# Seven-product steps for six more column pairs, and the gates kept on chip, in a hybrid decoder block

## The chip, the cores and the metric

The kernel runs on one core of one Trainium2 chip. The metric is the device time of one execution in microseconds (us); the core has a matrix engine (TensorE, PE in the rows, PEld for its weight loads), VectorE (DVE), ScalarE (ACT), GpSimd (POOL) and SyncE (SP), whose queue issues nearly all weight transfers.

## The reference, cut to what matters

The block takes `x` of 256 rows by 2048 columns, all in float32.

```python
h = rmsnorm(x, norm_mix)
q, k, v, o_pre, i_pre, f_pre, cb, cc, cx, ga, gb = split_columns(h @ w_in)
hm = mlstm_chunkwise(q, k, v, i_pre + b_igate, f_pre + b_fgate)      # 8 heads of 256 columns
hm = hm * rsqrt(mean(hm * hm, per head) + EPS) * mh_norm
hm = sigmoid(o_pre) * hm
y_a = hm @ w_branch_a
y_b = (cb * causal_depthwise_conv(cc * cx, conv_w)) @ w_branch_b
merged = sigmoid(ga) * y_a + sigmoid(gb) * y_b
x = x + merged @ w_out
hf = rmsnorm(x, norm_ffn)
x = x + (silu(hf @ w_gate) * (hf @ w_up)) @ w_down
return rmsnorm(x, norm_final)
```

`o_pre`, `ga` and `gb` are 2048 columns wide each, and so are the weights of both branches and of the output projection, with 2048 rows each.

## The kernel before, in words

**Chunks.** All weights pass through one ring in chunks of 1 MB, 128 partitions of 2048 values. SP loads chunk after chunk into four slots of `w_raw`; a load waits until VectorE has split the chunk four places earlier (`lo_split`). ScalarE copies a chunk to `w_hi` in the type fp32r (`split`, the copy at L580), VectorE subtracts it from the raw values to get `w_lo` (`split`, L1029). Both have two slots: ScalarE may write a slot when TensorE has finished the first part of its work on the chunk two places earlier (`hi_used`), VectorE when TensorE has finished all of it (`lo_used`).

**Plain chunks.** A float32 product is made of three: `x_hi w_hi`, `x_lo w_hi`, `x_hi w_lo`. A chunk holds either four row blocks of 128 by 512 columns (`project`, L1666, L1667, L1675) or two row blocks by 1024 columns. With 256 rows of x, either is 8 block products of 128 x 128 by 512 columns, so 24 matmuls: 16 with `w_hi`, then 8 with `w_lo`.

**Seven-product steps.** `front_step` (L1759, L1760, L1766) works on pairs of 512-column blocks, a pair having 8 steps. In the steps named in `FRONT_S` it makes the 8 block products out of 7 (a Strassen-like scheme), so 21 matmuls. That needs sums of the tiles of x (`x_form_hi`, `x_form_lo`, made once by `x_forms` on VectorE) and sums of the weight blocks of that chunk: VectorE's `sums_of` (L1130, L1133, L1135), then ScalarE's copy to `t_hi_x`, then VectorE's `t_lo_x` (L1155). The products land in eight PSUM banks (`FRONT_BANKS`). `front_extra` (L1180 to L1185) takes four of them in step 7, once ScalarE has copied the bank P1; `front_main` (L1192) takes the other four after the pair, and ScalarE's `front_out` scales the four results with the rows' factor into `qk` or `vx`. Steps are called by pair and number below: (1, 2) is step 2 of pair 1.

**Order before.** Chunks follow this order: two plain blocks of q and k; three pairs (`FRONT` = 3: the rest of q and k, then v) with 2, 3 and 3 seven-product steps; four turns `conv_turn` of 12 plain chunks, one for each 512-column block of cb, cc, cx, with the recurrence of two heads woven in; four plain blocks of `o_pre`, 4 chunks each; four turns `merge_turn` of 16 plain chunks (ga, branch a, gb, branch b); four blocks of the output projection; then the FFN and the down projection, which use seven-product steps too. The last transposes and taps of the convolution (`turn_p`, `p_taken`, `conv_0`, `conv_1`, `cu_high`, `conv_low`) run during the first block of `o_pre`. There the Sigmoid of each block goes to `nat`, VectorE forms the gated heads `hm` (L1354), TensorE turns them (`turn_block`, L1684) and `group_hi` and `group_lo` store `hmT_hi`, `hmT_lo`. The order of each engine's work is written out by hand; a wait blocks everything behind it on its engine.

In the pairs ScalarE's loop has this body, which the change touches:

```python
if j < 2 * BC - 1:
    front_split(p, j + 1)
...
if p > 0 and j == 0:
    front_out(p - 1)
```

`front_out(p - 1)` waits for `front_main(p - 1)` of VectorE.

Of the kernel before, what the change touches and what calls it, by code (L numbers as in the profile page):

```python
# [29 lines left out]
ALU = mybir.AluOpType  # L30
# [20 lines left out]
FRONT_S = ((4, 6), (2, 4, 6), (2, 4, 6))  # L51
# [50 lines left out]
def hybrid_block(nc, x, norm_mix, w_in, b_igate, b_fgate, conv_w, mh_norm, w_branch_a, w_branch_b,  # L102
# [29 lines left out]
    G_MERGE = G_O + NB * BC  # L132
    G_OUT = G_MERGE + 4 * NB * BC
# [20 lines left out]
    with ExitStack() as ctx:  # L154
# [20 lines left out]
        hmT_hi, hmT_lo = at("hmT_hi", [P, KC, SEQ], F32R, R3), at("hmT_lo", [P, KC, SEQ], F32R, R3 + AT)  # L175
# [14 lines left out]
        actT = at("actT", [P, FC, SEQ], F32, Z)  # L190
# [14 lines left out]
        fT_hi, fT_lo = at("fT_hi", [P, KC, SEQ], F32R, R3), at("fT_lo", [P, KC, SEQ], F32R, R3 + AT)  # L205
# [18 lines left out]
        hm = at("hm", [P, RT, COLS], F32, s + 4096)  # L224
# [65 lines left out]
        def sem(name):  # L290
# [44 lines left out]
                                                                 sem("x_form_hi_done"), sem("x_form_lo_done"))  # L335
        xp1_out, x_extra, x_main = sem("xp1_out"), sem("x_extra"), sem("x_main")
# [17 lines left out]
        FRONT_AT = (G_QK + 2 * BC, G_V, G_V + 2 * BC)  # L354
        FRONT = len(FRONT_AT)
# [36 lines left out]
        def _(sp):  # L392
# [39 lines left out]
            for p, c in enumerate((C_QK + 2 * COLS, C_V, C_V + 2 * COLS)):  # L432
                for j in range(2 * BC):
                    chunk = Chunk(FRONT_AT[p] + j)
                    sp.wait_ge(lo_split, chunk.count(1 - RAW_SLOTS))
                    sp.dma_start(w_raw[:, chunk.raw, :].rearrange("p (k n) -> p k n", k=2),
                                 w_in_k[:, 2 * j:2 * j + 2, c:c + 2 * COLS]).then_inc(raw_landed[chunk.raw], 16)
            with sp.Fori(0, NB) as i:
# [60 lines left out]
        def _(pool):  # L499
# [50 lines left out]
            rstd_of(h_mean, ss[:], ss[:], rstd[:], 1, DV, h_rstd)  # L550
            pool.wait_ge(x1_summed, 1)
# [27 lines left out]
        def _(act):  # L579
# [22 lines left out]
            def group_hi(n, dst, k0, step, scale_at=None):  # L602

                act.wait_ge(grp_turned, n)
                src = bank_kt(4)
# [77 lines left out]
            def front_split(p, j):  # L683

                if j in FRONT_S[p]:
# [4 lines left out]
                    copy(t_hi_x[:], t_raw_x[:].rearrange("p u n -> p (u n)")).then_inc(t_hi_done, 1)  # L690
                split(Chunk(FRONT_AT[p] + j))

            def front_out(p):

                act.wait_ge(x_main, (p + 1) * X_MAIN)
                for b in range(2):
                    for r in range(RT):
                        if p == 0:
# [1463 lines left out]
```

## Time and profile before

| | |
|---|---|
| median of 3 runs | 1724.8 us (1724.71 to 1725.06) |
| the profiled execution's own time | 1725.06 us |
| its span, first to last instruction | 1723.2 us |
| TensorE busy | 1711.2 us, 99% of the span, 7724 matmuls |
| VectorE busy | 1181.7 us, 69% |
| ScalarE busy | 858.8 us, 50% |
| GpSimd busy | 61.7 us, 4% |
| mean granted TensorE clock | 0.998 |

The profile was taken in one execution; 1.9 us of its own time lie outside the span. Busy shares are averages over stages with different limits. TensorE's matmuls are pipelined: one is recorded as 0.39 us long while the next starts 0.23 us after it, so its rate is read from the distance between starts.

### The profile page before, as it was taken

The page shows a single profiled execution, that of the slowest core. Times are in us where ns is not written, and L with a number is a line of the kernel's source. Part 1 is how long each engine was busy: PE and PEld are TensorE (multiplying, and loading weights), DVE is VectorE, ACT ScalarE, POOL GpSimd, SP SyncE. Part 2 cuts the span into 40 slices and gives each one's busy share as a digit, 9 for nine tenths or more (in the row PEclk, how much of TensorE's full clock was granted, in tenths as well). Part 3 has the DMA queues.
Part 4 walks back from the last instruction along what each step waited for, and adds up shares of the span by engine and source line. Part 5 has one row for each costly group of instructions (what it writes and reads, how often), then busy time and mean ns, then how long its engine had stood idle before and what let it go on. Part 6 is the DMA issues. An engine that isn't in the chain of part 4 may idle for free.

```text
span 1723.2 us, 20654 instructions
## 1 busy us (share of the span) xinstructions
PE 1711.2 (99%) x7724; PEld 1418.9 (82%) x7724; DVE 1181.7 (69%) x991; ACT 858.8 (50%) x756; POOL 61.7 (4%) x60
## 2 busy tenths in 40 slices
PE   9999999999999999999999999999999999999998
PEld 8888888888888888888888888888888888888886
DVE  5888555566565544444445579888888888898887
ACT  6555544454444434333333556555555555555564
POOL 1000010101000000000000000000000000230000
PEclk9999999999999999999999999999999999999999
DMA  8555545554555555555556556655556565556653
GB/s 281 188 190 200 190 160 188 171 167 161 181 180 186 177 194 193 195 195 195 195 195 233 182 171 197 199 201 200 201 196 196 197 199 201 184 195 222 221 195 118
DMA packets 151465, 331.29 MB, mean 192 GB/s; under 512 B 8720, under 2 KB 8816, under 8 KB 151024
## 3 DMA queue, kind: packets, MB, share of 16 engines
q1 hardware_dynamic: 151264, 329.98, 56.6%
q8 instruction: 38, 0.62, 0.1%
q10 hardware_dynamic: 144, 0.52, 0.1%
q14 instruction: 19, 0.16, 0.0%
HBM read 328.38 MB, written 2.10 MB: 192 GB/s over the span
## 4 chain that ended last, share of the span: by engine, by line
PE 98%; issue 0%; DVE 0%; ACT 0%; DMA 0%; SPq 0%; POOLq 0%; DVEq 0%; POOL 0%; ACTq 0%
PE ps L1666 16%; PE ps L1667 16%; PE ps L1675 16%; PE ps L1989 9%; PE ps L1991 9%; PE ps L1995 9%; PE ps L2070 4%; PE ps L2071 4%; PE ps L2075 4%; PE ps L1759 2%; PE ps L1760 2%; PE ps L1766 2%; PE ps L1684 1%; PE ps L1945 1%; PE ps L1796 0%
## 5 line engine op out<-in xcount | busy, mean ns | idle before, releaser
L1029 DVE TENSOR_TENSOR w_lo<-w_raw,w_hi 128x2048 fp32r<-128x2048 f32 x308 | 709.7, 2307 | 239.8 <-ACT w_hi L580 237.1
L580 ACT ACTIVATE w_hi<-w_raw 128x2048 fp32r<-128x2048 f32 (+1 forms) x309 | 588.8, 1910 | 311.3 <-PE ps L1667 171.8
L1666 PE MATMUL ps<-w_hi,xT_hi 128*128 128x512 f32 x832 | 329.7, 396 | 0.0
L1667 PE MATMUL ps<-w_hi,xT_lo 128*128 128x512 f32 x832 | 324.0, 389 | 0.0
L1675 PE MATMUL ps<-w_lo,xT_hi 128*128 128x512 f32 x832 | 205.6, 389 | 0.0
L1675 PEld LDWEIGHTS ps<-w_lo,xT_hi 128*128 128x128 f32 x832 | 156.2, 188 | 32.4
L1666 PEld LDWEIGHTS ps<-w_hi,xT_hi 128*128 128x128 f32 x832 | 156.3, 188 | 32.2
L1667 PEld LDWEIGHTS ps<-w_hi,xT_lo 128*128 128x128 f32 x832 | 156.3, 188 | 31.5
L1989 PE MATMUL ps<-w_hi,fT_hi 128*128 128x512 f32 x396 | 156.3, 395 | 0.0
L1991 PE MATMUL ps<-w_hi,fT_lo 128*128 128x512 f32 x396 | 154.3, 390 | 0.0
L580 ACT ACTIVATE t_hi<-t_raw 128x1536 fp32r<-128x1536 f32 x45 | 66.9, 1486 | 110.4 <-PE ps L1995 87.8
L1995 PE MATMUL ps<-w_lo,fT_hi 128*128 128x512 f32 x396 | 120.1, 389 | 0.0
L2070 PE MATMUL ps<-w_hi,a_hi 128*128 128x512 f32 x280 | 109.0, 389 | 0.0
L2071 PE MATMUL ps<-w_hi,a_lo 128*128 128x512 f32 x280 | 108.9, 389 | 0.0
L1995 PEld LDWEIGHTS ps<-w_lo,fT_hi 128*128 128x128 f32 x396 | 74.3, 188 | 15.4
L1989 PEld LDWEIGHTS ps<-w_hi,fT_hi 128*128 128x128 f32 x396 | 74.4, 188 | 15.0 <-issue 0.3
L1991 PEld LDWEIGHTS ps<-w_hi,fT_lo 128*128 128x128 f32 x396 | 74.4, 188 | 14.8
L1397 DVE TENSOR_TENSOR t_lo<-t_raw,t_hi 128x1536 fp32r<-128x1536 f32 x33 | 57.9, 1756 | 23.0 <-ACT t_hi L580 22.9
L2075 PE MATMUL ps<-w_lo,a_hi 128*128 128x512 f32 x280 | 73.3, 389 | 0.1
L1989 PE MATMUL ps<-w_hi,form_hi 128*128 128x512 f32 x176 | 68.6, 390 | 0.0
L1991 PE MATMUL ps<-w_hi,form_lo 128*128 128x512 f32 x176 | 68.5, 389 | 0.0
L2075 PEld LDWEIGHTS ps<-w_lo,a_hi 128*128 128x128 f32 x280 | 52.5, 188 | 11.4 <-DVE w_lo L1029 0.5
(295 smaller groups left out, 2345.8 us busy)
## 6 DMA issues: line engine op xcount, KB each, us to landing
w_raw<-in_w_in SPq DMA_DIRECT2D x127, 1024.0 KB, 5.1
w_raw<-in_w_gate SPq DMA_DIRECT2D x88, 512.0 KB, 3.8
w_raw<-in_w_up SPq DMA_DIRECT2D x88, 512.0 KB, 4.6
w_raw<-in_w_down SPq DMA_DIRECT2D x44, 1024.0 KB, 5.3
w_raw<-in_w_branch_a SPq DMA_DIRECT2D x16, 1024.0 KB, 5.0
w_raw<-in_w_branch_b SPq DMA_DIRECT2D x16, 1024.0 KB, 5.0
w_raw<-in_w_out SPq DMA_DIRECT2D x16, 1024.0 KB, 5.1
xn<-in_x SPq DMA_DIRECT2D x4, 512.0 KB, 8.4
```

The source lines that it names most:

```text
L580: copy = lambda o, i, **kw: nc.scalar.activation(o, i, ACT.Copy, **kw)
L1029: V.tensor_tensor(w_lo[:, chunk.split, :], w_raw[:, chunk.raw, :], w_hi[:, chunk.split, :].bitcast(F32), ALU.subtract).then_inc(lo_split, 1)
L1397: V.tensor_tensor(t_lo[:], t_raw[:].rearrange("p u n -> p (u n)"), t_hi[:].bitcast(F32), ALU.subtract).then_inc(t_lo_done, 1)
L1666: T.matmul(ps[:, banks + r, :], rows(hi, k, r), w, start=(q == 0 and k == 0), stop=False)
L1667: last = T.matmul(ps[:, banks + r, :], rows(lo, k, r), w, start=False, stop=False)
L1675: last = T.matmul(ps[:, banks + r, :], rows(hi, k, r), w, start=False, stop=(q == BC - 1 and k == KB - 1))
L1989: T.matmul(ps[:, banks[name], :], tile_of(0, k, tile), moving(0, u), start=begins(name) and part is own(name)[0], stop=False)
L1991: return T.matmul(ps[:, banks[name], :], tile_of(1, k, tile), moving(0, u), start=False, stop=False)
L1995: return T.matmul(ps[:, banks[name], :], tile_of(0, k, tile), moving(1, u), start=False, stop=final(name) and part is own(name)[-1])
L2070: T.matmul(ps[:, banks[name], :], tile(0, t), moving(0, u), start=start, stop=False)
L2071: return T.matmul(ps[:, banks[name], :], tile(1, t), moving(0, u), start=False, stop=False)
L2075: return T.matmul(ps[:, banks[name], :], tile(0, t), moving(1, u), start=False, stop=stop)
```

## The change: what it does

The four blocks of `o_pre`, `ga` and `gb` become six pairs (numbers 3 to 8) that run through `front_step`, two for each. Pair 3 has seven-product steps 4 and 6; pairs 4 to 8 have steps 2, 4 and 6. The 16 + 64 chunks of the old blocks become 48 chunks in pairs and 32 plain ones of the branches, now without loops in the program. The sums of x for the later pairs are made again by GpSimd (`late_x_forms`), split by ScalarE in pair 3 at j = 2 and by VectorE at j = 3. ScalarE applies the Sigmoid in `front_out`; the eight gate blocks of ga and gb stay in SBUF. VectorE gates the heads in place in `vx` during pairs 4 and 5 (`gate_heads`), and TensorE turns them (`turn_heads`) in the first four plain chunks, which are of branch b. `front_out` is cut in two halves, issued at j = 1 and 2 of the next pair, for the three old pairs as well (after the third: at j = 0 and 1 of the convolution). Several tensors get other places in SBUF.

```diff
-FRONT_S = ((4, 6), (2, 4, 6), (2, 4, 6))
+FRONT_S = ((4, 6), (2, 4, 6), (2, 4, 6), (4, 6)) + ((2, 4, 6),) * 5
+FRONT = 3
...
@@ SyncE
-            with sp.Fori(0, NB) as i:
-                load_block(G_O, i, BC, w_in_k, C_O + i * COLS)
-            with sp.Fori(1, NB + 1) as i:
-                for n, (w, c) in enumerate(((w_in_k, C_GA), (w_a_k, 0), (w_in_k, C_GB), (w_b_k, 0))):
-                    load_block(G_MERGE + (n - 4) * BC, i, 4 * BC, w, i * COLS + (c - COLS))
+            for n, c in enumerate((C_O, C_O + 2 * COLS, C_GA, C_GA + 2 * COLS, C_GB, C_GB + 2 * COLS)):
+                load_x_pair(FRONT + n, c)
+            for i in range(NB):
+                for n, w in enumerate((w_b_k, w_a_k)):
+                    load_block(G_Y + (2 * i + n) * BC, 0, 0, w, i * COLS)
@@ GpSimd, after rstd_of(h_mean, ...)
+            def late_x_forms():
+                nc.gpsimd.tensor_tensor(out=late_pick[:], in0=steps(xT_hi), in1=steps(xT_lo),
+                                        op=ALU.add).then_inc(late_form_step, 1)
+                pool.wait_ge(late_form_step, 1)
+                for n in range(2):
+                    nc.gpsimd.tensor_tensor(out=late_form_raw[:, :, n, :], in0=late_pick[:, :, 0, n * P:(n + 1) * P],
+                                            in1=late_pick[:, :, n, P:2 * P] if n else late_pick[:, :, 0, P:2 * P],
+                                            op=ALU.subtract).then_inc(late_form_step, 1)
+                ... (two more of the same size)
@@ ScalarE
-            def front_out(p):
+            def front_out(p, b):
                 act.wait_ge(x_main, (p + 1) * X_MAIN)
...
+                    last = nc.scalar.activation(dst, src, ACT.Copy if p < FRONT else ACT.Sigmoid,
+                                                scale=r_x[:, 0, r:r + 1])
...
-                    if p > 0 and j == 0:
-                        front_out(p - 1)
+                    if p > 0 and j in (1, 2):
+                        front_out(p - 1, j - 1)
...
+            for p in range(FRONT, PAIRS):
+                for j in range(2 * BC):
+                    if j < 2 * BC - 1:
+                        front_split(p, j + 1)
...
+                    if p == FRONT and j == 0:
+                        p_taken(NB - 1)
+                    if p == FRONT and j == 2:
+                        cu_high(NB - 1)
+                        act.wait_ge(late_form_step, 5)
+                        copy(late_forms[0][:], late_form_raw[:]).then_inc(x_form_hi_done, 1)
+                    if p > FRONT and j in (1, 2):
+                        front_out(p - 1, j - 1)
@@ VectorE
+            def gate_heads(n, b, r):
+                dve.wait_ge(act_out, A_O + 2 * n + b + 1)
...
+                for k in range(2):
+                    h = 4 * n + 2 * b + k
+                    part = vx[:, r, h, 0:DV]
+                    last = V.scalar_tensor_tensor(out=part, in0=part, scalar=rstd[:, r * H + h:r * H + h + 1],
+                                                  in1=c_o[b][:, r, k * DV:(k + 1) * DV], op0=ALU.mult, op1=ALU.mult)
...
+            for p in range(FRONT, PAIRS):
+                for j in range(2 * BC):
+                    if j == FRONT_S[p][-1] + 1:
+                        front_extra(p)
+                    if j > 0 and j + 2 in FRONT_S[p]:
+                        front_sums(p, j + 2)
+                    if p == FRONT and j == 3:
+                        dve.wait_ge(x_form_hi_done, 2)
+                        V.tensor_tensor(late_forms[1][:], late_form_raw[:], late_forms[0][:].bitcast(F32),
+                                        ALU.subtract).then_inc(x_form_lo_done, 1)
+                    if j < 2 * BC - 1:
+                        front_split(p, j + 1)
...
+                    if p in (FRONT + 1, FRONT + 2) and 3 <= j < 7:
+                        gate_heads(p - FRONT - 1, (j - 3) // 2, (j - 3) % 2)
+                    if p == FRONT and j < 3:
+                        (conv_0, conv_1, conv_low)[j](NB - 1)
+                front_main(p)
@@ TensorE
+            for p in range(FRONT, PAIRS):
+                for j in range(2 * BC):
...
+                    if p > FRONT and j == 0:
+                        pe.wait_ge(x_extra, p * X_EXTRA)
+                    if p > FRONT and j == FRONT_S[p][0]:
+                        pe.wait_ge(x_main, p * X_MAIN)
+                    front_step(p, j)
+                    if p == FRONT and j == 0:
+                        turn_p(NB - 1)
+            for i in range(NB):
+                for j in range(2 * BC):
+                    n, q = j // BC, j % BC
...
+                    project(Chunk(G_Y + i * 2 * BC + j), 2 * n, *((cuT_hi, cuT_lo), (hmT_hi, hmT_lo))[n], q)
...
+                        turn_heads(q, 4 + q % 2 * 2)
+                    if i > 0 and j == 1:
...
+                        turn_block(gate_a[i - 1], 4, grp_turned)
```

## Rows read from the trace of the kernel before

**Rows 1.** The page: busy time of each engine; the group of ScalarE's chunk copies.

```profile
PE 1711.2 (99%) x7724; PEld 1418.9 (82%) x7724; DVE 1181.7 (69%) x991; ACT 858.8 (50%) x756; POOL 61.7 (4%) x60
...
L580 ACT ACTIVATE w_hi<-w_raw 128x2048 fp32r<-128x2048 f32 (+1 forms) x309 | 588.8, 1910 | 311.3 <-PE ps L1667 171.8
```

**Rows 2.** Waits of TensorE: us in total, times, longest.

```profile
PE ps L1759 <- issue: 0.8, 2, 0.4
```

**Rows 3.** Windows: us; busy of PE, PEld, DVE, ACT, POOL; clock; DMA; GB/s.

```profile
482.10:926.50 444.40, 444.40 (x1994) 368.61 (x1993) 220.14 (x139) 180.44 (x131) 0.00 (x0) 1.00 0.55 191
134.80:176.80 42.00, 41.58 (x184) 34.15 (x183) 35.48 (x29) 22.16 (x17) 0.00 (x0) 1.00 0.57 197
1037.00:1079.40 42.40, 42.40 (x190) 34.90 (x189) 39.39 (x32) 25.96 (x18) 0.00 (x0) 1.00 0.65 217
```

**Rows 4.** Timeline of TensorE, first matmuls of steps (0, 4), (0, 5), (0, 6).

```profile
82.74 0.39 PE L1759 MATMUL ps<-w_hi,xT_hi 128*128 128x512 f32 x1
...
87.50 0.39 PE L1759 MATMUL ps<-w_hi,xT_hi 128*128 128x512 f32 x1
...
92.94 0.39 PE L1759 MATMUL ps<-w_hi,xT_hi 128*128 128x512 f32 x1
```

**Rows 5.** Timeline of TensorE, end of step (1, 1), start of (1, 2).

```profile
112.21 1.97 PE L1766 MATMUL ps<-w_lo,xT_hi 128*128 128x512 f32 x8
114.60 0.47 PE L1759 MATMUL ps<-w_hi,xT_hi 128*128 128x512 f32 x1 [0.42 <-issue]
114.91 0.40 PE L1760 MATMUL ps<-w_hi,xT_lo 128*128 128x512 f32 x1
```

**Rows 6.** Timeline of ScalarE in steps (1, 1) and (1, 2).

```profile
108.75 2.56 ACT L580 ACTIVATE qk<-c_x,r_x 128x512 f32<-128x512 f32 x4 [5.25 <-DVE c_x L1192]
111.22 1.47 ACT L580 ACTIVATE t_hi_x<-t_raw_x 128x1536 fp32r<-128x1536 f32 x1
```

**Rows 7.** Timeline of VectorE from step (0, 7) to (1, 2).

```profile
98.79 0.69 DVE L1180 TENSOR_TENSOR c_x<-ps,c_x 128x512 f32<-128x512 f32 x1 [3.17 <-ACT c_x L580]
...
101.45 2.28 DVE L1029 TENSOR_TENSOR w_lo<-w_raw,w_hi 128x2048 fp32r<-128x2048 f32 x1
103.65 1.22 DVE L1130 TENSOR_TENSOR t_raw_x<-w_raw 128x1024 f32<-128x1024 f32 x1
...
106.24 2.48 DVE L1192 TENSOR_TENSOR c_x<-ps,c_x 128x512 f32<-128x512 f32 x4
108.63 2.28 DVE L1029 TENSOR_TENSOR w_lo<-w_raw,w_hi 128x2048 fp32r<-128x2048 f32 x1
112.72 1.76 DVE L1155 TENSOR_TENSOR t_lo_x<-t_raw_x,t_hi_x 128x1536 fp32r<-128x1536 f32 x1 [1.81 <-ACT t_hi_x L580]
```

**Rows 8.** Timeline of TensorE, `w_lo` part of the third chunk of `o_pre`.

```profile
497.39 1.98 PE L1675 MATMUL ps<-w_lo,xT_hi 128*128 128x512 f32 x8
```

**Rows 9.** Timeline of VectorE in the first blocks of `o_pre`.

```profile
496.72 1.23 DVE L1246 TENSOR_TENSOR uT<-uT,cbT 128x1024 f32<-128x1024 f32 x1
497.86 2.28 DVE L1029 TENSOR_TENSOR w_lo<-w_raw,w_hi 128x2048 fp32r<-128x2048 f32 x1
...
507.49 1.68 DVE L1354 SCALAR_TENSOR_TENSOR hm<-vx,rstd,nat 128x256 f32<-128x256 f32 x4 [4.00 <-ACT nat L597]
```

**Rows 10.** Timeline of ScalarE in the same place.

```profile
497.98 1.07 ACT L580 ACTIVATE cuT_hi<-uT 128x1024 fp32r<-128x1024 f32 x1 [3.40 <-DVE uT L1246]
```

**Rows 11.** Timeline of GpSimd, before `o_pre` and in the down projection.

```profile
476.05 2.92 POOL L520 TENSOR_TENSOR rstd<-ss,half 128x16 f32<-128x16 f32 x1
...
1484.46 0.74 POOL L562 TENSOR_TENSOR down_form_raw<-actT 128x256 f32<-128x256 f32 x1
1485.28 0.46 POOL L565 TENSOR_TENSOR down_form_raw<-down_form_raw,actT 128x128 f32<-128x128 f32 x1
...
1498.03 2.19 POOL L562 TENSOR_TENSOR down_form_raw<-actT 128x256 f32<-128x256 f32 x1 [11.31 <-DVE down_form_lo L1553]
1500.30 2.39 POOL L565 TENSOR_TENSOR down_form_raw<-down_form_raw,actT 128x128 f32<-128x128 f32 x1
```

More of the change, by code:

```diff
@@ L760, in conv_turn @@
                     split(c.next())
-                    if j == 0 and first:
-                        front_out(FRONT - 1)
+                    if j in (0, 1) and first:
+                        front_out(FRONT - 1, j)
                     if j == 0 and not first:
@@ L807, in _ @@
                 conv_turn(i)
-            for n in range(NB):
-                for q in range(BC):
-                    c = Chunk(G_O + n * BC + q)
-                    split(c.next())
-                    if n == 0:
-                        if q == 0:
-                            p_taken(NB - 1)
-                        if q == 2:
-                            cu_high(NB - 1)
-                    if n > 0 and q == 1:
-                        group_hi(GRP_HM + n, hmT_hi, (n - 1) * KB, 0, V_MH)
-                if n > 0:
-                    act.wait_ge(hm_done, n)
-                else:
-                    act.wait_ge(p_turned, NB)
-                take(c, n % 2, nat[:], ACT.Sigmoid)
@@ L828, in merge_turn @@
-            def merge_turn(i):
-                first = starts(i)
-                for j in range(4 * BC):
-                    c = Chunk(G_MERGE + j, i, 4 * BC)
-                    split(c.next())
-                    if j == 1:
-                        if first:
-                            group_hi(GRP_M, hmT_hi, (NB - 1) * KB, 0, V_MH)
-                        else:
-                            group_hi(i + GRP_M, mT_hi, (i - 1) * KB, 0)
-                    if j == 3:
-                        if not first:
-                            act.wait_ge(dve_out, V_MERGE + i * 2)
-                        take(c, 0, gate[:], ACT.Sigmoid)
-                    if j == 3 + 2 * BC:
-                        act.wait_ge(dve_out, V_MERGE + 1 + i * 2)
-                        take(c, 0, gate[:], ACT.Sigmoid)
@@ L851, in pair_split @@
+            for i in range(NB):
+                for j in range(2 * BC):
+                    split(Chunk(G_Y + i * 2 * BC + j).next())
+                    if i == 0 and j in (1, 2):
+                        front_out(PAIRS - 1, j - 1)
+                    if i == 0 and j < BC:
+                        group_hi(GRP_HM + j + 1, hmT_hi, j * KB, V_MH, 4 + j % 2 * 2)
+                    if i > 0 and j == 1:
+                        group_hi(GRP_M + i, mT_hi, (i - 1) * KB)
             def pair_split(j, i):
@@ L891, in _ @@
                     if n == 0 and q == 1:
[L892 removed]
+                        group_hi(GRP_F, mT_hi, (NB - 1) * KB)
                     if n > 0 and q == 0:
@@ L1379, in merge_turn @@
                 dve.wait_ge(dve_out, V_MERGE + 2 + i * 2)
-                V.tensor_tensor(merged[:], merged[:], prod[:], ALU.add).then_inc(m_done, 1)
-            merge_turn(0)
-            with dve.Fori(1, NB) as i:
-                merge_turn(i)
+                V.tensor_tensor(gate_a[i][:], gate_a[i][:], gate_b[i][:], ALU.add).then_inc(m_done, 1)
             def pair_split(j, i):
```

290 lines of the change are left out of this document (147 added, 143 removed).

## The prediction, on record before the changed kernel ran

> **What bounds the kernel now.** The page comes first: TensorE is busy for 1711.2 of 1723.2 us, in 7724 matmuls, and no other engine for more than 69% [rows 1]. The waits of TensorE come next, since a busy engine may still be slowed by others: what bears on this change is one entry, two waits that start at L1759, so in the pairs [rows 2]. The windows say whether the region to be changed is different: from 482.1 to 926.5 us, where `o_pre` and the branches are computed, TensorE is busy all the time at granted clock 1.00 (the higher of its two levels, 2.4 GHz), and VectorE for 220 of 444 us [rows 3]. So the time goes by the number of matmuls, and work added on VectorE is free until it makes TensorE wait. For the price of a matmul I take starts, not durations: the seven-product step (0, 4) runs from 82.74 to 87.50, 4.76 us for 21 matmuls, and the plain step (0, 5) to 92.94, 5.44 us for 24 [rows 4]. Both are 0.2267 us for one matmul, whichever tiles it reads.
>
> **Matmuls removed.** 80 chunks stay 80 chunks, and 17 of them lose 3 matmuls each: 51 x 0.2267 = 11.56 us, all on the path. Transposes stay as many: 8 for `turn_p`, 32 for the heads, 32 for `merged`. That sum is the firm part.
>
> **The two waits in the old pairs.** In step (1, 1) the last eight matmuls start at 112.21 and every 0.2267 us after it, so that step (1, 2) could start at 114.02. It starts at 114.60, and its second matmul comes 0.31 instead of 0.23 us later: 0.66 us lost [rows 5]. ScalarE shows why: it waited 5.25 us for VectorE's last results of pair 0, copied them for 2.56 us in `front_out`, and only then made the `t_hi` of step (1, 2), at 111.22, and behind it the chunk's `w_hi` [rows 6]. The changed order puts `t_hi` and `w_hi` of step 2 ahead of `front_out`. The sums of the weights are done at 106.24 [rows 7], so `t_hi` ends at 107.7 and, with 1.91 us for a chunk [rows 1], `w_hi` at 109.6, long before 114.02. VectorE then goes on at 110.9 instead of idling 1.81 us [rows 7]. The wait is there twice [rows 2]; both go: 1.32 us. Bounds: 0, if VectorE and not the order were to blame, and 1.32.
>
> **VectorE in the new pairs.** A whole old pair costs it 35.48 us [rows 3]. The gated heads add 8 operations to pairs 4 and 5; four of them took 1.68 us [rows 9], so 3.4 us, together 38.8 us. A pair with three seven-product steps has 183 matmuls, 41.5 us. That is a load of 94%; a turn of the FFN runs at 39.39 of 42.4 us, 93%, without holding TensorE up [rows 2, 3]. The order inside a pair matters more than the sum. From the old pair: `front_extra` can start 0.9 us after TensorE is done with step 6 (98.79) and ends at 101.45; then come a split, the sums (103.65 to 106.24), `front_main` (2.48 us) and the split of step 1, which ends at 110.9 [rows 7]. TensorE starts (1, 1) at 108.58 (one plain step before 114.02) and wants `w_lo` 16 matmuls later, at 112.2: 1.3 us to spare. In the steps after it each split is ready with more than that. The gating comes when VectorE idled in the old pair (1.81 us at once at 112.72, 3.17 us before 98.79). I take 0 for pairs 4 to 8; the upper bound is 0.66 us for each, the wait of rows 5.
>
> **Where pair 3 begins.** Here three things meet on VectorE: the last taps of the convolution, the sums for step (3, 4), and the `lo` part of the new forms. The chunks keep their places up to there. The third chunk's `w_lo` part starts at 497.39 [rows 8], so (3, 3) runs from 499.20 to 504.64 and wants `w_lo` at 502.83. VectorE ends the last convolution product so that its next operation starts at 497.86 [rows 9]. Before, this was the split of (3, 3); now the sums are first, 2.59 us (103.65 to 106.24), to 500.45, and the split ends at 502.73 [rows 7], 0.1 us before it is wanted. Then `conv_low`, of the size of the product at 496.72, with 1.14 us from start to start [rows 9], to 503.8; the forms' `lo`, as large as `t_lo` and so 1.76 us [rows 7], to 505.55. ScalarE is earlier: `cu_high` ends at 499.05 [rows 10], the forms' copy and `t_hi` take 1.47 each [rows 6] and `w_hi` 1.91 [rows 1], to 503.9. So (3, 4) starts 0.91 us late, plus 0.08 us for the start as in rows 5: first wait, 1.0 us. Its `w_hi` part is 14 matmuls, 3.17 us, so `w_lo` and `t_lo` are wanted at 508.8. VectorE ends `t_lo` at about 507.2 and the split at 509.4: second wait, 0.7 us. What is late next: the sums of step (3, 6) end at 512.0 and the split of (3, 5) at 514.2; TensorE, at (3, 5) from about 511.1, wants it at 514.7. From there VectorE is in front again. Together 1.7 us. Bounds: 0, if each overlaps a little better, and 6.1 us, if none of the added work ahead of that split (2.59 + 1.76 + 1.76) is hidden.
>
> **GpSimd's new forms.** One operation over 1536 columns and four over 384, after `rstd`, which ends at 478.97 [rows 11]. ScalarE asks for them at 499.05. Cheap, with VectorE out of the way, 256 columns took 0.74 and 128 took 0.46 us [rows 11], so 2.2 ns for a column and 0.18 us for an operation: 7.7 us, done at 487. If each also waits for one split of VectorE, 5 x 2.28 more, they end at 498. I take 0. Rows 11 show the dear end too: the 128 columns take 2.39 us while VectorE is at its SBUF operations. The Trainium skill, SBUF — State Buffer, Who interferes with whom, has the rule that speaks against moving such work: a VectorE instruction with two SBUF inputs and a GpSimd instruction that reads SBUF exclude each other for the whole instruction. By that the trace agrees (2.39 against 0.46 us), and five such waits give the 498 above, so the sum would stay.
>
> **The rest, at nothing.** The Sigmoids are as many as before, 24, and ScalarE has half of each window free [rows 3]. The weights of a pair are 8.4 MB in 41.5 us, 202 GB/s, where the FFN's window moved 217 with TensorE busy throughout [rows 3]. In the first plain chunks ScalarE has 1.91 us of copy in each 5.44 us [rows 1, 4], and beside it the two halves of `front_out` (2.56 us together [rows 6]) and the four groups of `group_hi`; a group stored late holds TensorE only from the fifth chunk on, where branch a begins to read the turned heads.
>
> **Sum.** 1725.06 (the profiled execution) - 11.56 - 1.32 + 1.7 = 1713.9 us. The median of the runs is 0.26 us below that execution, so **1713.6 us**.
>
> **Rivals.** *The start of pair 3 is covered.* VectorE's margin there is tenths; if the forms' `lo` comes in time, 1725.06 - 12.88 = 1712.2, median 1711.9 us. Against it: the operations are in series and none can be left out. 15%. *The feeders are late in every pair.* If VectorE, at 94%, and not `front_out`'s place causes the waits of rows 5, the old two stay and the five later pairs have one each: -11.56 + 1.7 + 5 x 0.66 = -6.6, 1718.2 us. For it: the margin of 1.3 us in step 1. Against it: ScalarE's 5.25 us of idling ahead of `front_out` [rows 6]. 15%. *GpSimd is late, and the kernel slower.* At the dearest row, 2.39 us for 128 columns, the 3072 columns of the forms take 57.4 us and end at 536.3. ScalarE, held in pair 3 at j = 2 with the copies of (3, 4) behind it, needs 4.85 us more, so TensorE starts at 541.2 instead of 504.6: 36.5 us lost, 1725.06 - 12.88 + 36.5 = 1748.7, median 1748.4 us. It decides from forms that end at 512.7 (no gain left) and is a measurable loss from 516.1. Against it: VectorE is busy half of that stretch [rows 3], and the cheap rows are a fifth of the dear one. 3%. The forecast as worked out has 57%; 10% lies between it and the second rival, with a longer wait at pair 3.
>
> **How the numbers follow.** Likeliest: 1713.6. Range: the first rival with half a microsecond below, 1711.2, up to 1717.5, which takes in most of the 6.1 us bound at pair 3 and leaves out the two rivals above it, 18%. Within 0.2% (3.4 us), about what a measurement of this kernel can tell from no change, lies only GpSimd's lateness in part: faster 95%, same 2%, slower 3%.
>
> **What would show it.** Right: 7673 matmuls; no wait of TensorE at steps (1, 2) and (2, 2); one of about 1.0 and one of about 0.7 us at (3, 4), put down to VectorE's forms and splits; starts 0.2267 us apart and clock 1.00 throughout the pairs; GpSimd's forms done before 499. Wrong: waits at step 1 or 2 of pairs 4 to 8, starts further apart in steps that read `late_form_hi`, transposes of the heads that wait for `hm_done`, or group stores in the branch chunks that hold TensorE.

## The result, and the profile after

| | before | changed |
|---|---|---|
| median | 1724.76 us (1724.56 to 1725.06, 4 runs) | 1713.72 us (1713.38 to 1714.92, 4 runs) |
| the profiled execution's own time | 1725.06 us | 1713.56 us |
| its span | 1723.2 us | 1711.7 us |
| matmuls | 7724 | 7673 |

The changed kernel takes 0.9937 of the time before (95% interval 0.992 to 0.9954), so it is 11.0 us faster. The forecast was 1713.6 us, and it rested on a sum of three terms. A sum can come out right with wrong terms, so the two traces are compared stage by stage.

The page of the changed kernel, its line of busy times; [rows 1] has the one of before:

```profile
PE 1698.0 (99%) x7673; PEld 1407.2 (82%) x7673; DVE 1281.9 (75%) x1108; ACT 888.0 (52%) x780; POOL 71.3 (4%) x65
```

TensorE has 51 matmuls fewer. VectorE has 100 us more work and ScalarE 29 us more, and neither has become the bound: the page says so, but only a stage's waits prove it. The waits of TensorE in the changed kernel (line waited at, whom for, us in total, times, longest):

```profile
PE ps L1754 <- POOL half L523: 1.7, 1, 1.7
PE ps L1713 <- ACT w_hi L616: 1.7, 1, 1.7
PE ps L1814 <- ACT w_hi L616: 0.9, 1, 0.9
PE ps L1759 <- DMA vec_rows<-in_conv_w: 0.7, 1, 0.7
PE ps L1821 <- DVE w_lo L1064: 0.4, 1, 0.4
```

The first, second and fourth lie in the first 30 us, in code that is as before, and vary from run to run by half a microsecond and more. L1814 and L1821 are `front_step` after the change. The two waits of [rows 2] are gone, and in their place stand one of 0.9 and one of 0.4 us. The view of TensorE over time says where (start, duration, operation, what ended the idle time):

```profile
191.14 0.61 PE L1886 MATMUL ps<-ident,r_a 8*128 8x8 f32 x4
...
500.99 2.08 PE L1821 MATMUL ps<-w_lo,xT_hi 128*128 128x512 f32 x8
503.96 0.47 PE L1814 MATMUL ps<-w_hi,xT_hi 128*128 128x512 f32 x1 [0.90 <-ACT w_hi L616]
504.27 0.40 PE L1815 MATMUL ps<-w_hi,xT_lo 128*128 128x512 f32 x1
...
507.01 0.39 PE L1815 MATMUL ps<-late_t_hi,xT_lo 128*128 128x512 f32 x1
507.75 0.50 PE L1821 MATMUL ps<-w_lo,xT_hi 128*128 128x512 f32 x1 [0.35 <-DVE w_lo L1064]
...
912.95 0.39 PE L1713 MATMUL ps<-w_hi,mT_hi 128*128 128x512 f32 x1
```

Both waits are at step (3, 4). Idle times in such rows are short by the modelled ends of the matmuls, so starts are compared: 507.01 to 507.75 is 0.74 us where 0.227 is the rule, and the start after it (508.09) comes 0.34 us later where 0.227 is the rule, so the wait cost 0.51 + 0.11 = 0.62 us. The first one, counted in the same way from the last matmul of the eight, which starts at 502.68, cost 1.06 + 0.08 = 1.14 us. Another 0.08 us is lost at the `w_lo` part at 500.99, whose second matmul comes 0.31 us after the first. Together 1.84 us.

With the first and last row of this fence (the first transposes of the head columns, where the convolution begins, and the first matmul of the output projection) and with the first matmul of `o_pre` the kernel falls into stages. The same landmarks are at 193.01, 481.98 and 924.46 us before, and at 191.14, 480.14 and 912.95 us after:

| stage, us | before | after | difference |
|---|---|---|---|
| first weight matmul (10.29, 9.79) | | | -0.50 |
| to the convolution: plain blocks, pairs 0 to 2 | 182.72 | 181.35 | -1.37 |
| convolution | 288.97 | 289.00 | +0.03 |
| `o_pre`, branches, gates | 442.48 | 432.81 | -9.67 |
| from the output projection to the last matmul | 789.96 | 790.03 | +0.07 |

The third difference is -51 x 0.2267 + 1.84 = -9.72, and 0.05 from many small steps. Of the -1.37, the two waits of [rows 5] are 1.32. The 0.50 us at the top is no part of the change: in the executions of this document the first weight matmul starts anywhere from 9.14 to 10.29 us. Without it the stages add up to -10.94 us, beside -11.04 for the medians.

### The profile page after: what moved, and what is told of

It reads as the page before. It is cut to its first block, busy times and chain, and to the rows that moved or that the text cites. A ratio compares the mean times of both kernels' runs of the same rounds, so it can differ in the third digit from the quotient of the medians.

```text
span 1711.7 us, 20301 instructions
## 1 busy us (share of the span) xinstructions
PE 1698.0 (99%) x7673; PEld 1407.2 (82%) x7673; DVE 1281.9 (75%) x1108; ACT 888.0 (52%) x780; POOL 71.3 (4%) x65
## 4 chain that ended last, share of the span: by engine, by line
PE 97%; DVE 1%; issue 1%; ACT 0%; DMA 0%; SPq 0%; POOLq 0%; DVEq 0%; POOL 0%; ACTq 0%
PE ps L1713 11%; PE ps L1714 11%; PE ps L1722 11%; PE ps L2032 9%; PE ps L2034 9%; PE ps L2038 9%; PE ps L1821 7%; PE ps L1814 7%; PE ps L1815 7%; PE ps L2113 4%; PE ps L2114 4%; PE ps L2118 4%; PE ps L1739 1%; PE ps L1988 1%; DVE w_lo L1064 0%
## 5 line engine op out<-in xcount | busy, mean ns | idle before, releaser
L1713 PE MATMUL ps<-w_hi,xT_hi 128*128 128x512 f32 x448 | 179.6, 401 | 1.7 <-ACT w_hi L616 1.7
L1714 PE MATMUL ps<-w_hi,xT_lo 128*128 128x512 f32 x448 | 174.6, 390 | 0.0
L1814 PE MATMUL ps<-w_hi,xT_hi 128*128 128x512 f32 x426 | 165.9, 389 | 0.9 <-ACT w_hi L616 0.9
L1815 PE MATMUL ps<-w_hi,xT_lo 128*128 128x512 f32 x426 | 165.7, 389 | 0.0
L1821 PE MATMUL ps<-w_lo,xT_hi 128*128 128x512 f32 x426 | 112.5, 390 | 0.4 <-DVE w_lo L1064 0.4
L1722 PE MATMUL ps<-w_lo,xT_hi 128*128 128x512 f32 x448 | 110.7, 389 | 0.0
L1713 PEld LDWEIGHTS ps<-w_hi,xT_hi 128*128 128x128 f32 x448 | 84.2, 188 | 19.3 <-ACT w_hi L616 1.9
L1722 PEld LDWEIGHTS ps<-w_lo,xT_hi 128*128 128x128 f32 x448 | 84.1, 188 | 17.5
L1714 PEld LDWEIGHTS ps<-w_hi,xT_lo 128*128 128x128 f32 x448 | 84.2, 188 | 16.8
L1814 PEld LDWEIGHTS ps<-w_hi,xT_hi 128*128 128x128 f32 x426 | 80.0, 188 | 17.8 <-issue 1.3
L1821 PEld LDWEIGHTS ps<-w_lo,xT_hi 128*128 128x128 f32 x426 | 79.9, 188 | 17.5 <-DVE w_lo L1064 1.0
L1815 PEld LDWEIGHTS ps<-w_hi,xT_lo 128*128 128x128 f32 x426 | 80.0, 188 | 16.5
```

What stands on the lines that cost most here:

```text
L1713: T.matmul(ps[:, banks + r, :], rows(hi, k, r), w, start=(q == 0 and k == 0), stop=False)
L1714: last = T.matmul(ps[:, banks + r, :], rows(lo, k, r), w, start=False, stop=False)
L1722: last = T.matmul(ps[:, banks + r, :], rows(hi, k, r), w, start=False, stop=(q == BC - 1 and k == KB - 1))
L1814: T.matmul(ps[:, banks[name], :], tile(0, t), moving(0, u), start=begins, stop=False)
L1815: last = T.matmul(ps[:, banks[name], :], tile(1, t), moving(0, u), start=False, stop=False)
L1821: last = T.matmul(ps[:, banks[name], :], tile(0, t), moving(1, u), start=False, stop=ends)
```

## The experiments

Each table or sentence gives the median of the kernel's own runs beside the ratio to the kernel before on the same chip. "C to D" is the stage from the first matmul of `o_pre` to the first of the output projection, 432.81 us in the changed kernel and 442.48 before; "A to B" is that from the first weight matmul to the convolution. A to B also holds the last of the first loads, which cost TensorE up to 1.2 us more in some executions (1.11 us at 15.39 in that with `front_out` whole and first), so it is compared only where they did not.

### The changed kernel again

> The changed kernel itself, on the chip of the runs sent with it: 1713.7 us, with the two waits at (3, 4) that together cost 1.8 us.

1713.98 us (1713.17 to 1714.17, 5 runs), ratio 0.9936 (0.9923 to 0.995). The waits at (3, 4) cost 1.14 and 0.62 us and A to B is 181.34 us, so both are properties of the order of work and not of one execution.

### Only the place and halves of front_out, in the kernel before

```diff
-def front_out(p):
+def front_out(p, b):
...
-    if p > 0 and j == 0:
-        front_out(p - 1)
+    if p > 0 and j in (1, 2):
+        front_out(p - 1, j - 1)
...
-    if j == 0 and first:
-        front_out(FRONT - 1)
+    if j in (0, 1) and first:
+        front_out(FRONT - 1, j)
```

> The kernel before with one part of the change alone: front_out in two halves, at j = 1 and 2 of the next pair (j = 0 and 1 of the convolution). If front_out's place caused the waits at steps (1, 2) and (2, 2), both go and the time falls by 1.3 to 1.4 us, to 1723.4, with t_hi of step (1, 2) ending about 5 us earlier. If VectorE's load caused them, they stay and the time stays at 1724.8.

1723.35 us (1722.62 to 1724.01, 11 runs), ratio 0.9994 (0.9985 to 1.0003). Over whole runs the effect is no larger than the uncertainty. The stage shows it: A to B falls from 182.72 to 181.33 us, by 1.39, and C to D stays at 442.48. ScalarE and TensorE of this kernel, in pair 1:

```profile
105.44 1.49 ACT L580 ACTIVATE t_hi_x<-t_raw_x 128x1536 fp32r<-128x1536 f32 x1 [2.85 <-DVE t_raw_x L1134]
```

```profile
111.30 1.98 PE L1765 MATMUL ps<-w_lo,xT_hi 128*128 128x512 f32 x8
113.11 0.39 PE L1758 MATMUL ps<-w_hi,xT_hi 128*128 128x512 f32 x1
```

`t_hi_x` no longer stands behind 2.56 us of `front_out`; it starts as soon as the sums are there, 4.9 us earlier than in [rows 6] when both are counted from the first weight matmul (9.39 and 10.29), and step (1, 2) starts 1.81 us = 8 x 0.2267 after the eight matmuls of [rows 5] began: no wait.

### The changed kernel with front_out whole and first again

```diff
-if p > 0 and j in (1, 2):
-    front_out(p - 1, j - 1)
+if p > 0 and j == 0:
+    front_out(p - 1, 0)
+    front_out(p - 1, 1)
```

(and the same for `p > FRONT` in the loop of the new pairs).

> The changed kernel with front_out whole at j = 0 again in all pairs. If its place is the cause, TensorE waits 0.66 us at step 2 of pairs 1, 2 and 4 to 8, seven times, and the time is 4.6 us above the changed kernel's 1713.7, at 1718.3. If VectorE's load were the cause in the old kernel, the place would change nothing: 1713.7.

1718.33 us (1718.04 to 1719.04, 5 runs), ratio 0.9964 (0.995 to 0.9977). C to D grows by 3.43 us, 0.69 for each of pairs 4 to 8, and the profile counts seven waits at the start of step 2. The waits of TensorE, and its rows at (4, 2):

```profile
PE ps L1816 <- issue: 2.9, 7, 0.4
```

```profile
536.13 1.97 PE L1823 MATMUL ps<-w_lo,xT_hi 128*128 128x512 f32 x8
538.52 0.47 PE L1816 MATMUL ps<-w_hi,xT_hi 128*128 128x512 f32 x1 [0.41 <-issue]
```

ScalarE in the same stretch:

```profile
532.67 2.57 ACT L741 ACTIVATE c_o<-c_o,r_x 128x512 f32<-128x512 f32 x4 [3.95 <-DVE c_o L1232]
```

536.13 to 538.52 is 2.39 us where 1.81 is the rule. It is the picture of [rows 5, 6] in every pair. So this small edit of the diff carries 0.65 to 0.69 us for each of seven pairs, 1 and 2 among them; without it the new pairs would have given back a third of their gain (3.43 of 9.67 us). The entry names "issue", which is what a wait looks like when the profile finds no event for it; ScalarE's row beside it names the cause.

### Pairs 4 to 8 with two seven-product steps

```diff
-FRONT_S = ((4, 6), (2, 4, 6), (2, 4, 6), (4, 6)) + ((2, 4, 6),) * 5
+FRONT_S = ((4, 6), (2, 4, 6), (2, 4, 6), (4, 6)) + ((4, 6),) * 5
```

> The changed kernel with steps 4 and 6 alone in pairs 4 to 8: 12 seven-product steps instead of 17. If a step is worth exactly its 3 matmuls and nothing is given back, the time rises by 5 x 0.68 = 3.4 us to 1717.1, with the same two waits at (3, 4). If VectorE held the pairs up, fewer steps would give part of it back and the rise would be under 2.5 us.

1717.37 us (1716.31 to 1718.35, 5 runs), ratio 0.9958 (0.9944 to 0.9972), 7688 matmuls. C to D grows by 3.41 us; 15 matmuls of 0.2267 us are 3.40. So the third step of these pairs gives its whole price back even in pairs 4 and 5, where VectorE has most to do. If VectorE had been costing TensorE something there, taking 5 sums and splits away would have saved some of it.

### The new sums of x made and split earlier

GpSimd makes the forms during the convolution; ScalarE copies them and VectorE splits them at the top of pair 3.

```diff
-            pool.wait_ge(h_squared, RT * H)
-            rstd_of(h_mean, ss[:], ss[:], rstd[:], 1, DV, h_rstd)
...
+            pool.wait_ge(staged, 2 * NB)
             late_x_forms()
+            pool.wait_ge(h_squared, RT * H)
+            rstd_of(h_mean, ss[:], ss[:], rstd[:], 1, DV, h_rstd)
...
                     if p == FRONT and j == 0:
+                        act.wait_ge(late_form_step, 5)
+                        copy(late_forms[0][:], late_form_raw[:]).then_inc(x_form_hi_done, 1)
                         p_taken(NB - 1)
...
+                    if p == FRONT and j == 0:
+                        dve.wait_ge(x_form_hi_done, 2)
...
+                        V.tensor_tensor(late_forms[1][:], late_form_raw[:], ...)
```

(and both are taken out of their old places, j = 2 and j = 3).

> The changed kernel with GpSimd's forms made right after the last staging of q and k (about 70 us earlier), ScalarE's copy of them ahead of p_taken and VectorE's lo part ahead of conv_0, where both engines were idle. If the waits at (3, 4) come from VectorE's chain of operations in series, taking 1.7 us out of it removes the first wait and all but about 0.1 us of the second: 1.7 us less than the changed kernel, 1712.0. If they come from something else (the landing of the chunk, ScalarE, PSUM banks), the time stays at 1713.7.

1712.22 us (1711.81 to 1713.49, 5 runs), ratio 0.993 (0.9916 to 0.9943). C to D falls by 1.77 us to 431.04. VectorE of this kernel:

```profile
484.01 1.75 DVE L1410 TENSOR_TENSOR late_form_lo<-late_form_raw,late_form_hi 128x1536 fp32r<-128x1536 f32 x1
```

The 1.75 us now lie in the time in which VectorE waits for ScalarE anyway (3.45 us of that wait are left, up to 489.21), and at 501.98, where the changed kernel has them, comes `late_t_lo`. TensorE starts step (3, 4) 1.91 us after the `w_lo` part of (3, 3) and waits no more. The edit moves three things at once (GpSimd's forms, ScalarE's copy, VectorE's subtraction); that the two waits of 1.76 us together hang on VectorE's operation of 1.75 us is read from the order in which TensorE's waits ended, told in the part on the prediction.

### As that, with the sums for step (3, 4) first as well

```diff
-if j > 0 and j + 2 in FRONT_S[p]:
+if j > 0 and j + 2 in FRONT_S[p] and not (p == FRONT and j + 2 == FRONT_S[p][0]):
     front_sums(p, j + 2)
...
+                        front_sums(p, FRONT_S[p][0])      # pair 3, j == 0, behind the split of the forms
```

> The kernel with early forms (e4), and VectorE's weight sums of step (3, 4) ahead of conv_0 too, in the place where it still idles for 3.45 us. They take 2.6 us out of the chain ahead of step (3, 4). If early forms left nothing but hundredths there (0.08 us at the w_lo part of (3, 3)), the time from the first matmul of pair 3 to the first of the output projection falls from 431.04 us by 0.1 us, and the median does not move beyond its noise: 1712.1.

**1711.83 us** (1711.78 to 1712.43, 5 runs), ratio 0.9927 (0.9914 to 0.9941). C to D is 430.91 us, which is 442.48 - 51 x 0.2267 = 430.92: nothing of the 51 matmuls is lost. It is the fastest version of all that ran, though against the one before it only the stage tells (0.13 us), not the runs.

### An 18th seven-product step, (3, 2)

The same early forms; the sums for step 2 at j = 0, and `conv_1`, `conv_low` and `cu_high` moved to j = 3, 5 and 4.

```diff
-FRONT_S = ((4, 6), (2, 4, 6), (2, 4, 6), (4, 6)) + ((2, 4, 6),) * 5
+FRONT_S = ((4, 6), (2, 4, 6), (2, 4, 6)) + ((2, 4, 6),) * 6
```

> The kernel with early forms, and step (3, 2) a seven-product step too, its sums ahead of conv_0; conv_1 and conv_low go to j = 3 and 5, cu_high to j = 4. Three matmuls fewer, 0.68 us; against it t_hi of (3, 2) is made behind p_taken, so w_hi of that step ends about 0.5 us after TensorE wants it, and VectorE's split of (3, 5) about 0.2 us. So about even with the 1712.2 of early forms: 1712.0 to 1712.4. If neither wait appears, 1711.5.

1712.57 us (1711.98 to 1712.71, 5 runs), ratio 0.9928 (0.9915 to 0.9942), 7670 matmuls. C to D is 430.93 us, 0.11 less than with 17 steps and the forms early. TensorE at (3, 2):

```profile
490.80 1.98 PE L1824 MATMUL ps<-w_lo,xT_hi 128*128 128x512 f32 x8
493.22 0.47 PE L1817 MATMUL ps<-w_hi,xT_hi 128*128 128x512 f32 x1 [0.44 <-issue]
```

Three matmuls saved are 0.68 us; the step starts 2.42 us after the `w_lo` part before it instead of 1.81, and its second matmul 0.08 us late: 0.69 us. ScalarE has `p_taken` (`pT` and `uT`, from 487.34 to 489.69) ahead of this step's `late_t_hi`, as it had `front_out` in [rows 6], and its `w_hi` behind that; another order was not tried. The step pays nothing as long as the wait is there.

### More load on VectorE in pairs 4 to 8

The added operation, of 128 x 768, computes nothing that is used. By the windows the three take 2.2 to 2.4 us of a pair: 11.05 us over the five, and 38.05 - 35.66 = 2.39 in pair 7, where TensorE never waits.

```diff
+                    if p > FRONT and j in (3, 4, 5):
+                        dve.wait_ge(pad_step, 3 * (p - FRONT - 1) + j - 3)
+                        V.tensor_tensor(pad[:].rearrange("p (k t) -> p k t", k=3), xT_lo[:, 0:3, :].bitcast(F32),
+                                        xT_lo[:, 3:6, :].bitcast(F32), ALU.add).then_inc(pad_step, 1)
```

> The changed kernel with three more VectorE additions of 128x768 (about 0.9 us each, into an unused place) in each of pairs 4 to 8, at j = 3, 4 and 5. VectorE's sum in pairs 4 and 5 becomes 41.7 us of a pair's 41.5, in pairs 6 to 8 38.3 us. If only the sum counts, TensorE waits under 1 us in all: 1713.7 to 1714.7. If the order inside a pair counts (rival: VectorE late at 92% already), each of the five pairs has waits and the time is 1717 or more.

1715.18 us (1715.03 to 1715.48, 4 runs), ratio 0.9945 (0.9929 to 0.996). C to D grows by 1.19 us: a little more than the 1 us at most that was expected if only the sum counted, and far less than the 3.3 us of waits in every pair. Busy time in windows of one pair, first of the changed kernel (TensorE, its weight loads, VectorE, ScalarE, GpSimd, granted clock, DMA share, GB/s), then of this kernel for VectorE alone:

```profile
525.80:567.30 41.50, 41.50 (x185) 34.38 (x184) 38.60 (x37) 23.82 (x17) 0.00 (x0) 1.00 0.58 203
...
608.80:650.30 41.50, 41.50 (x185) 34.38 (x184) 35.66 (x29) 22.42 (x16) 0.00 (x0) 1.00 0.57 203
```

```profile
526.80:568.30 41.50, 39.52 (x39) 1.00 0.59 203
568.30:609.80 41.50, 40.55 (x40) 1.00 0.58 203
609.80:651.30 41.50, 39.05 (x32) 1.00 0.57 203
651.30:692.80 41.50, 38.05 (x32) 1.00 0.58 203
```

The changed kernel's VectorE is busy for 38.60 us in each of pairs 4 and 5 (predicted 38.8) and 35.66, 35.66 and 35.37 in those after, and TensorE is busy throughout. With the load TensorE waits at the start of pairs 5 and 6 and at the `w_lo` part of their step 1, about 0.5 us for each pair, and nowhere in pairs 7 and 8. TensorE and VectorE at the first such place:

```profile
565.24 1.98 PE L1826 MATMUL ps<-w_lo,xT_hi 128*128 128x512 f32 x8
567.19 0.50 PE L1819 MATMUL ps<-w_hi,xT_hi 128*128 128x512 f32 x1
```

```profile
566.44 0.69 DVE L1224 TENSOR_TENSOR c_o<-ps,c_o 128x512 f32<-128x512 f32 x1
```

The start at 567.19 follows the last operation of `front_extra`, which ends at 567.13; from there VectorE is behind, and the `w_lo` part at 576.56 follows the split that ends at 576.51. One wait of 0.66 us in each of the five pairs, the second rival's case, would be 3.3 us, and even with the load only 1.19 were measured. So in a window that is 94% full (39.05 of 41.5 us, pair 6) VectorE holds nobody up, and in those 95 and 98% full (pairs 4 and 5) it costs half a microsecond a pair. The windows understate what pairs 4 and 5 were given, 38.60 and 2.2 to 2.4 us more, some 41 us or 98 to 99%: part of it slips into the next window, and pair 6 shows 1.0 us more than pair 7.

### GpSimd ends late: six operations more

The added operations compute `late_pick` again; the result is the same.

```diff
+                for n in range(6):
+                    nc.gpsimd.tensor_tensor(out=late_pick[:], in0=steps(xT_hi), in1=steps(xT_lo),
+                                            op=ALU.add).then_inc(pad_step, 1)
+                    pool.wait_ge(pad_step, n + 1)
                 nc.gpsimd.tensor_tensor(out=late_pick[:], in0=steps(xT_hi), in1=steps(xT_lo),
```

> The changed kernel with GpSimd's first operation of the late forms (3.8 us) made six more times ahead of it, the same result. If GpSimd's end decides as worked out, the forms end at about 510.6, TensorE starts (3, 4) 4.85 us later, 11.5 us after the 503.96 of the changed kernel, and the second wait there goes: 10.9 us more, 1724.6, so the whole gain is gone with 23 us of work on an engine that is busy for 4% of the span. If the slack of 9.9 us seen in the changed kernel's trace is not real, or if ScalarE's block spreads to the chunks behind, more is lost.

1729.78 us (1729.51 to 1730.65, 6 runs), ratio 1.0031 (1.0019 to 1.0043): slower than before, and 5.2 us above what was expected. C to D is 449.08 us, 16.27 more than in the changed kernel. That was a miss, and the traces show what was left out. GpSimd and VectorE in the changed kernel:

```profile
477.09 3.82 POOL L572 TENSOR_TENSOR late_pick<-xT_hi,xT_lo 128x1536 f32<-128x1536 f32 x1
...
481.96 3.07 POOL L576 TENSOR_TENSOR late_form_raw<-late_pick 128x384 f32<-128x384 f32 x1
...
486.19 1.01 POOL L583 TENSOR_TENSOR late_form_raw<-late_form_raw,late_pick 128x384 f32<-128x384 f32 x1
```

```profile
481.77 2.39 DVE L1064 TENSOR_TENSOR w_lo<-w_raw,w_hi 128x2048 fp32r<-128x2048 f32 x1
489.17 1.67 DVE L1264 SCALAR_TENSOR_TENSOR uT<-pT,vecT,uT 128x256 f32<-128x256 f32 x4 [5.01 <-ACT uT L616]
...
501.96 1.75 DVE L1397 TENSOR_TENSOR late_form_lo<-late_form_raw,late_form_hi 128x1536 fp32r<-128x1536 f32 x1
```

And with six operations more, first the six together and then the third of them alone:

```profile
476.94 23.74 POOL L573 TENSOR_TENSOR late_pick<-xT_hi,xT_lo 128x1536 f32<-128x1536 f32 x6
...
484.41 5.44 POOL L573 TENSOR_TENSOR late_pick<-xT_hi,xT_lo 128x1536 f32<-128x1536 f32 x1
...
509.60 1.07 POOL L587 TENSOR_TENSOR late_form_raw<-late_form_raw,late_pick 128x384 f32<-128x384 f32 x1
```

```profile
480.29 1.41 DVE L1371 SCALAR_TENSOR_TENSOR nat<-ps,r_x,nat 128x512 f32<-128x512 f32 x2 [2.91 <-PE ps L1726]
481.61 4.87 DVE L1068 TENSOR_TENSOR w_lo<-w_raw,w_hi 128x2048 fp32r<-128x2048 f32 x1
489.01 11.94 DVE L1268 SCALAR_TENSOR_TENSOR uT<-pT,vecT,uT 128x256 f32<-128x256 f32 x4 [2.54 <-ACT uT L620]
500.88 5.50 DVE L1068 TENSOR_TENSOR w_lo<-w_raw,w_hi 128x2048 fp32r<-128x2048 f32 x1
```

The two engines do not slow each other in part; each stands still for whole operations of the other. Four VectorE products that take 1.67 us take 11.94: the last three start at 490.06, 493.72 and 497.33, each 0.13 us after a GpSimd operation, and take 3.6 to 3.7 us where one alone takes 0.48. A split of 2.28 us takes 5.50. It goes the other way too: GpSimd's operation at 484.41, begun during a VectorE split, takes 5.44 us where the shortest take 3.48, and in the changed kernel the 384 columns at 481.96 take 3.07 us where those at 486.19 take 1.01. VectorE's two `nat` operations, with one of their two tensors in PSUM, lose nothing: 1.41 us in the middle of the series, as in the kernel before at 482.28, where GpSimd is idle. This kernel's forms end 30.7 us after the first matmul of `o_pre` (510.67 - 479.98), exactly where the prediction saw the gain used up (512.7 - 481.98), and it is 5 us slower than that. The Trainium skill, SBUF — State Buffer, Who interferes with whom, says that one of the two holds the shared ports for a whole instruction and the other is blocked; the trace agrees, with 3.74 us for one product at 490.06 and 5.44 us for one GpSimd operation at 484.41. With VectorE's products at 0.48 us and GpSimd's operations at 3.5, taking turns lets VectorE work for 0.48 us in each 3.6.

TensorE then pays twice. Its rows, and the windows around them:

```profile
495.17 0.39 PE L1819 MATMUL ps<-w_hi,xT_lo 128*128 128x512 f32 x1
506.43 3.78 PE L1825 MATMUL ps<-w_lo,xT_hi 128*128 128x512 f32 x8 [10.88 <-DVE w_lo L1068]
510.01 0.45 PE L1818 MATMUL ps<-w_hi,xT_hi 128*128 128x512 f32 x1
...
517.06 3.63 PE L1825 MATMUL ps<-w_lo,xT_hi 128*128 128x512 f32 x8 [3.15 <-DVE w_lo L1068]
520.52 0.40 PE L1818 MATMUL ps<-w_hi,xT_hi 128*128 128x512 f32 x1
```

```profile
500.00:506.40 6.40, 0.00 (x0) 0.00 (x0) 6.40 (x3) 0.00 (x0) 6.24 (x3) 0.50 0.00 0
506.43:510.00 3.57, 3.57 (x8) 2.81 (x9) 3.57 (x4) 0.00 (x0) 3.41 (x4) 0.50 0.70 241
...
513.70:517.00 3.30, 0.20 (x1) 0.00 (x0) 3.27 (x4) 3.15 (x3) 0.00 (x0) 0.99 0.00 0
517.06:520.50 3.44, 3.44 (x8) 2.75 (x9) 3.41 (x3) 2.86 (x2) 0.00 (x0) 0.52 0.69 237
```

It waits 11.03 us (from 495.40, when the next matmul would have started) and 3.32 us (from 513.74), each time for `w_lo` and not for the forms. The granted clock is still 0.99 from 495.40 to 500.00, the first part of the first wait, and 0.50 in the rest of it. Over the eight matmuls after it the clock is 0.50, which is 1.2 GHz, and they take 3.58 instead of 1.81 us; over the eight after the second it is 0.52, and they take 3.46. The four terms are 11.03 + 3.32 + 1.77 + 1.65 = 17.77 us; less the 1.84 us that the changed kernel loses at pair 3 anyway, 15.9 of the 16.27.

### Two operations more: late or in the way?

The same edit with `range(2)`. In the six-operation kernel lateness and exclusion came together; two operations end before ScalarE asks for the forms, so only exclusion can cost.

> The changed kernel with two more of GpSimd's first operation (3.8 us each) instead of six. GpSimd's forms then end near 495, before ScalarE asks for them at 497.1. Theory A (only ScalarE's wait for the forms costs): nothing is lost, 1713.8. Theory B (GpSimd and VectorE keep each other out of SBUF, which the run with six more points to: four VectorE operations that take 1.67 us took 11.94): VectorE's taps and the splits of (3, 2) and (3, 3) between 489 and 495 each wait for the GpSimd operation under way, the series at pair 3 slips by 2 to 4 us, and the time is 1716 to 1718.

1717.75 us (1717.42 to 1718.91, 5 runs), ratio 0.9962 (0.9948 to 0.9975), C to D 3.59 us more than in the changed kernel, as the exclusion would have it (1716 to 1718) and not lateness (1713.8). TensorE's waits for `w_lo` in this kernel, then GpSimd, ScalarE and VectorE, a fence each:

```profile
PE ps L1825 <- DVE w_lo L1068: 3.4, 3, 1.9
```

```profile
493.86 1.07 POOL L587 TENSOR_TENSOR late_form_raw<-late_form_raw,late_pick 128x384 f32<-128x384 f32 x1
```

```profile
499.96 1.06 ACT L620 ACTIVATE cuT_hi<-uT 128x1024 fp32r<-128x1024 f32 x1 [6.95 <-DVE uT L1288]
```

```profile
482.04 4.88 DVE L1068 TENSOR_TENSOR w_lo<-w_raw,w_hi 128x2048 fp32r<-128x2048 f32 x1
489.44 4.62 DVE L1268 SCALAR_TENSOR_TENSOR uT<-pT,vecT,uT 128x256 f32<-128x256 f32 x4 [2.52 <-ACT uT L620]
493.98 3.10 DVE L1068 TENSOR_TENSOR w_lo<-w_raw,w_hi 128x2048 fp32r<-128x2048 f32 x1
```

The forms are done at 494.93. ScalarE, which is to copy them behind `cuT_hi`, waits 6.95 us for VectorE's `uT` and not for them: it asks for them at 500.9, and the kernel still loses 3.6 us. TensorE's starts say where: 1.42 us at the `w_lo` part of (3, 2), at 497.13, and 2.17 us at that of (3, 3), at 504.77; the waits at (3, 4) stay. VectorE's first split takes 4.88 instead of 2.39 us (hidden, it idles afterwards anyway), the four products 4.62 instead of 1.67, and the next split starts at 493.98 instead of 490.98 and takes 3.10 us. GpSimd costs by when it works, not by when it ends.

## Why the prediction came out right, step by step

**Matmuls removed, -11.56.** Right. 7673 matmuls, starts 0.2267 us apart with `late_form_hi` as with `xT_hi`, clock 1.00; the kernel with sums and forms early has the whole 11.57 us in C to D, and 15 matmuls put back cost 3.41 us.

**Two waits in the old pairs, -1.32.** Right: 0.66 us at each of the two steps is gone, and the stage is 1.37 us shorter. The edit alone gives -1.39 in the kernel before, and taken back it costs 0.69 us in each of the five new pairs. Its cause is the one read from [rows 6], the place of `front_out` on ScalarE and not VectorE's speed.

**Start of pair 3, +1.7.** Right in place, size and cause: 1.84 us, as 0.08 + 1.14 + 0.62 for the predicted 1.0 and 0.7. VectorE's chain was forecast to end the forms' `lo` at 505.55, 23.57 us after the stage begins at 481.98; it ended at 503.71, 23.57 us after 480.14. The first wait is still 0.15 us longer than worked out: TensorE starts 0.25 us after that end. The profile names a copy of ScalarE there, but that of this step's chunk ended at 502.03. The trace also records when TensorE's queue passed each semaphore of the step: that of the forms' `lo` (`pe.wait_ge(x_form_lo_done, ...)`, L1808) at 503.75 to 503.80, right behind VectorE's end at 503.71, then that of `late_t_hi` (L1809), long fulfilled, at 503.86 to 503.91, and the weight load at 503.93. So VectorE was the releaser. The 0.25 us are this passage, and most of the 0.15 are the second semaphore, passed 0.11 us after the first; at the second wait, which has one semaphore, the start follows 0.05 us after the split's end (507.70 to 507.75). The rival that this start is covered (1711.9 us) is what the kernel with forms early makes of it.

**Pairs 4 to 8, 0.** Right, for a load of 93% (38.60 of 41.5 us); the rival by which VectorE was late in each pair has nothing for it. How near its edge was, the added load shows: three operations more, 2.2 to 2.4 us, cost 0.5 us for each of the two fullest pairs.

**GpSimd, 0.** Right: the forms end at 487.20, which is 489.0 in the times of the kernel before, where 487 to 498 was worked out and 499.05 is when they are read. But the rival to it was worked out with the wrong mechanism. It priced only ScalarE's wait for late forms and put the break-even at forms that end at 512.7. The step that failed is "GpSimd is late": exclusion works in both directions, and the blocked VectorE delays TensorE's `w_lo` long before the forms are late. Loss begins within two more operations, which put the forms' end 7.5 us later, and with six the kernel is 0.3% slower than before. The change gets by because, of the 10.1 us of GpSimd's forms, VectorE idles in 6 (2.91 us up to 480.44, and from 484.16 on) and reads PSUM in 1.4, and the one split wholly inside them took 2.39 instead of 2.28 us: there it was GpSimd that stood still, for 2.1 us. So the term of nothing was right, but in part by luck: what protected it was the place of VectorE's gaps, which the prediction had only as a share of time ("busy half of that stretch"), and not the margin that it gave ScalarE. The 3% given to this rival went by a break-even that is wrong.

One sum of the prediction does not come out: half a microsecond below the first rival (1711.9) is 1711.4, not 1711.2. Nothing hangs on it.

## What to carry to other kernels

When one engine is busy all the time, price an edit in its instructions, then look for the step whose inputs come out of a serial chain on a feeder; here each wait, of 0.6 to 1.2 us, hung on one copy or one subtraction that could be made earlier, and making two of them earlier gave 1.9 us for no work taken away. An in-order engine should make what the bound engine reads next before it drains what is already finished. Work moved to GpSimd was free here only while VectorE idled or took one of its inputs from PSUM: ask in which of VectorE's gaps it falls, not only when it is done.

## What the runs showed of the hardware that was not expected

GpSimd and VectorE took turns on SBUF, one whole operation each, and a row of long GpSimd operations starved VectorE by that: its four products of 128 x 256 went from 1.67 to 11.94 us, one for each GpSimd operation of 128 x 1536 (3.5 us). Each side lost turns: one GpSimd operation took 5.44 us behind a VectorE split. After 11 us without a matmul TensorE worked at granted clock 0.50 (1.2 GHz), eight matmuls in 3.58 us, and nearly the same after a wait of only 3.3 us. In the long wait the clock had fallen well before the work came back (0.50 from 500.00 to 506.40); in the short one it is still 0.99 from 513.70 to 517.00 and 0.52 over the matmuls behind. Right behind the eight matmuls it was back (1.00 from 510.20 to 511.00 and from 520.50 to 525.00). A short wait has a small tail at full clock as well: the start after it comes 0.08 to 0.11 us late, which is to be added to each wait.
